# Head norm weights in the rotation tables, the query's root in the exponent, and the position bias loaded by GpSimd

## The chip, the cores and the metric

The kernel runs on one NeuronCore of one Trainium2 chip. All inputs and outputs lie in the chip's memory and are float32. The metric is the device time of one execution in microseconds (us), as the median of three runs. Five engines run their own instruction streams and meet only at semaphores: TensorE (PE), VectorE (DVE), ScalarE (ACT), GpSimd (POOL) and SyncE (SP). DMAs are issued by SP and by ACT in this kernel, and in the changed kernel by POOL too.

## The reference

Two blocks of layers over 256 tokens of width 2048. The first (a state space and linear attention mixer, then a squared ReLU MLP) is not touched. The second has two layers, each with three kinds of attention heads beside each other:

```python
def _layer(x, g_pre, g_post, w_in, a_qn, a_kn, ..., rpb, w_out, row, col):
    h = _rms_norm(x, g_pre)
    proj = einsum('bsd,de->bse', h, w_in)
    a_q, a_k, a_v, a_g, b_cq, b_ckv, b_kr, b_g, c_q, c_k, c_v, c_g = split(proj)
    # a: 8 query heads, 2 key heads of 128; norm by head, then rotation
    qa = _rope_axial(_rms_norm(a_q by head, a_qn), row, col)
    ka = _rope_axial(_rms_norm(a_k by head, a_kn), row, col)
    o_a = _dense_block_attention(qa, ka, a_v) * silu(a_g)
    # b: 4 heads whose queries, keys and values come out of two small latent rows
    o_b = _dense_block_attention(q_full, k_full, vb) * silu(b_g)
    # c: 4 heads, 16 neighbouring columns only, with a learnt position bias rpb
    o_c = _neighbourhood_attention(c_q, c_k, c_v, rpb) * silu(c_g)
    y = einsum('bse,ed->bsd', concat([o_a, o_b, o_c]), w_out)
    return x + _rms_norm(y, g_post)
```

`_rms_norm(x, g)` is x / sqrt(mean(x^2) + 1e-6) * g. `_rope_axial` turns the first half of a head's 128 numbers by the token's row and the second half by its column; in each half it is x * cos + (the two quarters exchanged) * (-sin, sin). The softmax is taken over scores times 128^-0.5.

## The kernel before

All large products are one stream of places. A place is a piece of 256 rows by 512 columns of a weight. SP loads it into one of four slots `raw`; ACT copies it to `w_hi` in a rounded format (L969), DVE subtracts to get the rest `w_lo` (L1600), and PE makes twelve matmuls of them (L939 to L941). Blocks of 512 output columns have 8 places in most weights, some have 1, 2, 6 or 16. ACT and DVE convert four places ahead of the place that they count (`AHEAD = 4`). A block's sums lie in two of four banks; they are taken out by ACT (L1507) and DVE (L2115, L2116) at place 3 of the next block (`DRAIN`), and PE may start the block after that only when both are done. SP loads into a slot again when DVE has split what was in it.

The rest of the work (attention, norms) stands beside this stream. Each piece of it is a generator that is started at a fixed place and goes on at fixed steps from there (`UNIT_STEP`, `ATTEND`), the same on every engine. So each engine's order is fixed in the program: at every place first the conversion four places ahead, then a drain if one is due, then the steps of the units beside. An engine that waits in such a step holds back all conversions behind it.

Each layer of the second block has four units, started 22 places apart: two of kind a (`grouped`, four query heads and one key head each, called a0 and a1 here), one of kind b (`latent_unit`) and one of kind c (`neighbour`).

In `grouped`, ACT issues seven loads: queries, key and value (L1421, L1423), the two norm weights (L1424, L1425), and the cos and sin tables (L1426, L1427). DVE waits for all of them at step 2, squares and sums (L1990, L1992, `root_of` L1609, L1611), ACT takes the roots (L983), at step 3 DVE multiplies by root and weight (L1998, L2000), at steps 4 and 6 it rotates one half of the tokens each (`rope`: L1982, L1985, L1987). At step 8 PE turns queries and keys (L789), at step 10 it makes the scores (L800), then DVE takes maxima (L2017, L2020), and ACT the exponentials (L1379).

In `neighbour`, ACT issues three loads of queries, keys and values (L1462), the load of the column mask (L1463) and sixteen loads of position bias out of a scratch tensor `skew` (L1467), each 64 partitions by four runs of 64 numbers, all at one place of its order. DVE waits for mask and bias at step 9 and adds them (L2091), and at step 10 adds the result to the scores (L2013). GpSimd has nothing to do but one memset near the start.

## Time and profile before

| | |
|---|---|
| median of 3 runs | 3020.25 us (3016.42 to 3022.92) |
| the profiled execution's own time | 3020.04 us |
| its span, first to last instruction | 3018.6 us |
| PE busy | 2932.7 us, 97% of the span |
| DVE busy | 1790.5 us, 59% |
| ACT busy | 1463.4 us, 48% |
| POOL busy | 0.4 us |
| mean granted TensorE clock | 0.984 of full speed |
| share of PE in the chain that ended last | 88% |

The busy figure of an engine counts instructions that run; an engine that issues DMAs or waits at a semaphore is idle by it. The clock is at one of two levels, full (1.0, 2.4 GHz) or half (0.5, 1.2 GHz), so a mean between them is a share of time at each. The profile's first 2190 us belong to the first block and the start of the second; the units of the first layer run from about 2212 to 2525 us, those of the second from about 2668 to 2980 us.

### The profile page before, as it was taken

To read this page: it belongs to the slowest core of one execution; us is meant where nothing else is said; L and a number is where in the kernel's file an instruction comes from. 1 tells how busy PE (TensorE), PEld (TensorE's weight loads), DVE (VectorE), ACT (ScalarE), POOL (GpSimd) and SP (SyncE) were. 2 spreads that over 40 slices of the span, in tenths; PEclk is the share of its full clock that TensorE was granted. 3 is DMA by queue.
4 is the path that set the end of the run, shared out by engine and by line. 5 is a ranking of instruction groups with operands and counts; after the bars stand their busy time and mean duration, and the time that the engine had idled before them with its cause. 6 is when DMAs were issued, how large, how long until landed. Compare 5 with 4: busy or idle time off the path is not lost.

```text
span 3018.6 us, 34820 instructions
## 1 busy us (share of the span) xinstructions
PE 2932.7 (97%) x13611; PEld 2428.2 (80%) x13611; DVE 1790.5 (59%) x2303; ACT 1463.4 (48%) x1997; POOL 0.4 (0%) x5
## 2 busy tenths in 40 slices
...
GB/s 209 223 210 224 229 220 228 236 228 225 251 224 229 230 227 257 276 217 163 222 196 177 202 176 201 171 196 136 240 204 199 195 213 175 234 207 191 207 202 164
DMA packets 348002, 634.99 MB, mean 210 GB/s; under 512 B 36653, under 2 KB 58413, under 8 KB 345534
## 3 DMA queue, kind: packets, MB, share of 16 engines
...
HBM read 582.99 MB, written 49.69 MB: 210 GB/s over the span
## 4 chain that ended last, share of the span: by engine, by line
PE 88%; DVE 5%; DMA 3%; ACT 2%; ACTq 2%; issue 1%; DVEq 0%
PE bank L939 27%; PE bank L941 27%; PE bank L940 27%; PE bank L601 2%; PE bank L800 1%; DMA arena<-in_sin 1%; DVE w_lo L1600 1%; PE bank L816 1%; PE bank L666 1%; ACTq L1467 1%; DMA raw<-in_w_out 1%; ACT w_hi L969 1%; PE bank L789 1%; DVE x_lo L1605 0%; PE bank L808 0%
## 5 line engine op out<-in xcount | busy, mean ns | idle before, releaser
L1600 DVE TENSOR_TENSOR w_lo<-raw,w_hi 128x1024 fp32r<-128x1024 f32 (+2 forms) x980 | 1159.4, 1206 | 732.2 <-ACT w_hi L969 721.6
L939 PE MATMUL bank<-w_lo,x_hi 128*128 128x512 f32 (+2 forms) x3920 | 1552.8, 396 | 34.1 <-DVE stage L2115 15.0
L941 PE MATMUL bank<-w_hi,x_lo 128*128 128x512 f32 (+2 forms) x3920 | 1529.6, 390 | 0.0
L940 PE MATMUL bank<-w_hi,x_hi 128*128 128x512 f32 (+2 forms) x3920 | 1529.5, 390 | 0.0
L969 ACT ACTIVATE w_hi<-raw 128x1024 fp32r<-128x1024 f32 (+2 forms) x980 | 993.3, 1045 | 735.7 <-PE bank L941 282.9
L939 PEld LDWEIGHTS bank<-w_lo,x_hi 128*128 128x128 f32 x3920 | 747.6, 191 | 190.9 <-DVE stage L2115 17.1
L941 PEld LDWEIGHTS bank<-w_hi,x_lo 128*128 128x128 f32 x3920 | 746.8, 191 | 152.7
L940 PEld LDWEIGHTS bank<-w_hi,x_hi 128*128 128x128 f32 x3920 | 747.6, 191 | 147.7 <-issue 2.9
L974 ACT ACTIVATE x_hi<-bank 128x512 fp32r<-128x512 f32 (+1 forms) x120 | 66.9, 589 | 329.2 <-PE bank L601 329.2
L1605 DVE TENSOR_TENSOR x_lo<-bank,x_hi 128x512 fp32r<-128x512 f32 (+1 forms) x120 | 78.1, 678 | 176.4 <-ACT x_hi L974 176.4
L601 PE MATMUL bank<-ident,arena 128*128 128x128 f32 x472 | 70.2, 288 | 29.8 <-DVE arena L1907 15.1
L601 PEld LDWEIGHTS bank<-ident,arena 128*128 128x128 f32 x472 | 58.6, 149 | 43.2 <-DVE arena L1907 18.3
L1675 DVE SCALAR_TENSOR_TENSOR arena<-arena 128x256 f32<-128x256 f32 x144 | 59.0, 478 | 45.3 <-ACT arena L1060 45.3
L983 ACT ACTIVATE arena<-arena 128x2 f32<-128x2 f32 (+2 forms) x38 | 7.5, 202 | 124.3 <-DVE arena L1611 103.2
L1385 ACT ACTIVATE arena<-bank 128x512 f32<-128x512 f32 x32 | 17.3, 593 | 59.0 <-PE bank L808 59.0
L800 PE MATMUL bank<-arena 128*128 128x256 f32 (+1 forms) x160 | 41.7, 398 | 0.0
L2030 DVE TENSOR_TENSOR arena<-arena 128x512 f32<-128x512 f32 x16 | 11.0, 688 | 50.6 <-ACT arena L1399 50.6
L1379 ACT ACTIVATE arena<-bank,arena 128x256 f32<-128x256 f32 x48 | 22.1, 482 | 33.6 <-DVE arena L2020 33.6
L1068 ACT ACTIVATE arena<-arena 128x128 f32<-128x128 f32 x128 | 38.2, 389 | 0.0
L800 PEld LDWEIGHTS bank<-arena 128*128 128x128 f32 (+1 forms) x160 | 27.8, 188 | 12.7 <-issue 10.0
L1369 ACT ACTIVATE arena<-bank 128x512 f32<-128x512 f32 (+3 forms) x34 | 16.4, 558 | 43.5 <-PE bank L789 43.5
L1055 ACT ACTIVATE arena<-bank 128x512 f32<-128x512 f32 x24 | 14.1, 586 | 42.9 <-PE bank L640 42.9
...
## 6 DMA issues: line engine op xcount, KB each, us to landing
...
raw<-in_w_up SPq DMA_DIRECT2D x128, 512.0 KB, 4.4
raw<-in_w_down SPq DMA_DIRECT2D x128, 512.0 KB, 4.6
...
```

What stands on the lines that cost most here:

```text
L601: op = pe.transpose(bank[b][:, k * P:(k + 1) * P], source[:, k * P:(k + 1) * P], ident[:, :])
L666: op = pe.matmul(bank[5 + t][:, h * SSD_P:(h + 1) * SSD_P], dec[:, t, h, :], xdt[:, t, h * SSD_P:(h + 1) * SSD_P], start=True, stop=True)
L800: op = pe.matmul(o_, qf(hh)[:, tokens(t)], kf(hh), start=(n == 0), stop=(n == len(parts) - 1))
L939: pe.matmul(o, x_hi[:, xk, tokens(t)], w_lo[:, r, k, 0:b.n], start=a, stop=False)
L940: pe.matmul(o, x_hi[:, xk, tokens(t)], w_hi[:, r, k, 0:b.n], start=False, stop=False)
L941: op = pe.matmul(o, x_lo[:, xk, tokens(t)], w_hi[:, r, k, 0:b.n], start=False, stop=z_)
L969: A(w_hi[:, p % SPLIT_RING, 0:b.per, 0:b.n], raw[:, p % RAW_RING, 0:b.per, 0:b.n], ACT.Copy).then_inc(*split_hi(p))
L974: return A(x_hi[:, x0:x0 + n, tokens(t)], full, ACT.Copy)
L1068: op = A(dec[:, t, h, :], dec[:, t, h, :], ACT.Relu, bias=gt[:, CS + t, h:h + 1], scale=-1.0)
L1600: TT(w_lo[:, p % SPLIT_RING, 0:b.per, 0:b.n], raw[:, p % RAW_RING, 0:b.per, 0:b.n], w_hi[:, p % SPLIT_RING, 0:b.per, 0:b.n].bitcast(F32), ...
L1605: return TT(x_lo[:, x0:x0 + n, tokens(t)], full, x_hi[:, x0:x0 + n, tokens(t)].bitcast(F32), ALU.subtract)
L1675: STT(cv[:, c, :], ut[:, c, w:w + S], cw[:, c, w:w + 1], cv[:, c, :], ALU.mult, ALU.add).then_inc(*ssd.dve("conv", g, w, c))
```

## The change

Four edits.

First, in `grouped` the norm weights are multiplied into cos and sin tables once per layer (`with_gain`, in unit a0 only), one pair of tables for queries and one for keys, and unit a1 uses them again. Norm weights, cos and sin are then loaded in a0 only; a1 loads queries, key and value.

Second, the queries are no longer multiplied by their root. The root of the queries is taken without the mean, so that it holds the factor 128^-0.5 too, and goes into the maxima (one `scalar_tensor_tensor` of 128x4) and into the exponentials' scale, which is now a number for each token and head. The keys are still multiplied by theirs. Keys are treated ahead of queries.

Third, the rotation's exchange (`rope`) is written by quarter, over all four heads at once: 4 instructions of 4x32 in place of 8 of 2x32 for queries, 4 of 32 in place of 2 of 2x32 for a key. The steps are one earlier: 3 and 5 in place of 4 and 6. Unit b uses the same function.

Fourth, mask and bias of `neighbour` are issued by GpSimd, after it has waited for the last readers and writers of that memory in unit b and for `skew`. DVE's wait is on their own semaphore.

```diff
@@ -434,6 +434,7 @@
+    bias_in = tally("bias_in", 16)
...
+            self.tables = {n: (room(NT, HD), room(NT, HD)) for n in "qk"}
@@ -1376,7 +1378,8 @@
-                    A(probs[t][:, hh, :], src, ACT.Exp, bias=small[:, t, hh:hh + 1], scale=1.0 if of_bias else scale,
+                    factor = 1.0 if of_bias else scale if scale else small[:, 4, t * UNIT_H + hh:t * UNIT_H + hh + 1]
+                    A(probs[t][:, hh, :], src, ACT.Exp, bias=small[:, t, hh:hh + 1], scale=factor,
                       accum_out=small[:, 2 + t, hh:hh + 1]).then_inc(*unit.act("exp", *key, t, hh))
@@ -1421,17 +1424,18 @@
-            act.dma_start(ga.gq, row_of(i["a_q_norm_2"][l], HD)).then_inc(*load[0]("unit", *key))
-            act.dma_start(ga.gk, row_of(i["a_k_norm_2"][l], HD)).then_inc(*load[0]("unit", *key))
-            act.dma_start(ga.cos, rows(i["cos128"])).then_inc(*load[0]("unit", *key))
-            act.dma_start(ga.sin, rows(i["sin128"])).then_inc(*load[0]("unit", *key))
+            if u == 0:
+                act.dma_start(ga.gq, row_of(i["a_q_norm_2"][l], HD)).then_inc(*load[0]("unit", *key))
+                act.dma_start(ga.gk, row_of(i["a_k_norm_2"][l], HD)).then_inc(*load[0]("unit", *key))
+                act.dma_start(ga.cos, rows(i["cos128"])).then_inc(*load[0]("unit", *key))
+                act.dma_start(ga.sin, rows(i["sin128"])).then_inc(*load[0]("unit", *key))
             yield UNIT_STEP["norm"] + 1
+            root_of(unit, (*key, "k"), small[:, 5, 0:2])
             root_of(unit, (*key, "q"), small[:, 4, :])
-            root_of(unit, (*key, "k"), small[:, 5, 0:2])
             yield UNIT_STEP["turn"]
             out_of_banks(("q", *key), ga.qt, (4, 5), HD)
             out_of_banks(("k", *key), ga.kt, (6,), HD)
-            yield from attend(key, UNIT_STEP["scores"], ga.probs, ga.pt, HD ** -0.5, False, ga.gate,
+            yield from attend(key, UNIT_STEP["scores"], ga.probs, ga.pt, None, False, ga.gate,
                               C2_AG + u * UW, KT + 4 * u)
 
@@ -1460,14 +1464,6 @@
-            act.dma_start(nu.mask, rows(i["window"])).then_inc(*load[1]("unit", *key))
-            for r in range(ROWS):
-                half = slice((r % 2) * GRID, (r % 2 + 1) * GRID)
-                for hh in range(C_H):
-                    act.dma_start(nu.bias[half, r // 2, hh * S:(hh + 1) * S].rearrange("p (a b) -> p a b", a=ROWS),
-                                  bass.AP(skew.tensor, (hh * DR + ROWS - 1 - r) * GRID * P + GRID - 1,
-                                          [[P - 1, GRID], [GRID * P, ROWS], [1, GRID]])).then_inc(
-                        *load[1]("unit", *key))
             yield UNIT_STEP["turn2"]
@@ -1978,30 +1974,35 @@
             xs, ts = split(x), split(tmp)
             ss = sin.rearrange("p (b s e) -> p b s e", b=2, s=2)
             for s in range(2):
-                for hh in range(heads):
-                    op = TT(ts[:, hh, :, s, :], xs[:, hh, :, 1 - s, :], ss[:, :, s, :], ALU.mult)
+                for b in range(2):
+                    op = TT(ts[:, :, b, s, :], xs[:, :, b, 1 - s, :], wide(ss[:, b, s, :].unsqueeze(1),
+                                                                           [P, heads, n // 4]), ALU.mult)
             op.then_inc(*unit.dve("shifted", *done))
             dve.wait_ge(*unit.dve.now)
             TT(x, x, wide(cos.unsqueeze(1), [P, heads, n]), ALU.mult).then_inc(*unit.dve("straight", *done))
             dve.wait_ge(*unit.dve.now)
             TT(x, x, tmp, ALU.add).then_inc(*unit.dve(*done))
 
-        def head_norm(key, x, n, g, stat, tmp):
+        def head_squares(key, x, stat, tmp):
             TT(tmp, x, x, ALU.mult).then_inc(*unit.dve("squares", *key))
             dve.wait_ge(*unit.dve.now)
             dve.tensor_reduce(stat, tmp, AX, ALU.add).then_inc(*unit.dve("sums", *key))
             dve.wait_ge(*unit.dve.now)
-            root_of(unit, key, stat, stat, HD, 1e-6)
-
-        def head_scale(key, x, n, g, stat):
-            dve.wait_ge(*unit.act["root", *key])
-            TT(x, x, wide(stat.unsqueeze(2), [P, n, HD]), ALU.mult).then_inc(*unit.dve("scaled", *key))
-            dve.wait_ge(*unit.dve.now)
-            TT(x, x, wide(g.unsqueeze(1), [P, n, HD]), ALU.mult).then_inc(*unit.dve("normed", *key))
+
+        def with_gain(l, name, gain):
+
+            cos, sin = ga.tables[name]
+            TT(cos, ga.cos, wide(gain.unsqueeze(1), [P, NT, HD]), ALU.mult).then_inc(*unit.dve("cos", l, name))
+            split = lambda a: a.rearrange("p t (b s e) -> p t b s e", b=2, s=2)
+            gains = gain.rearrange("p (b s e) -> p b s e", b=2, s=2)
+            for s in range(2):
+                for b in range(2):
+                    op = TT(split(sin)[:, :, b, s, :], split(ga.sin)[:, :, b, s, :],
+                            wide(gains[:, b, 1 - s, :].unsqueeze(1), [P, NT, HD // 4]), ALU.mult)
+            op.then_inc(*unit.dve("sin", l, name))
 
         def attend(key, at, probs, scale, bias, gate, x0):
             yield at
-            factor = 1.0 if bias is not None else scale
 
             def maxima(t):
                 top = small[:, t, 0:4]
@@ -2017,7 +2018,11 @@
                     op = dve.tensor_reduce(top[:, 2 * n:2 * n + 2], sc, AX, ALU.max)
                 op.then_inc(*unit.dve("top", *key, t))
                 dve.wait_ge(*unit.dve.now)
-                TS(top, top, -factor, None, ALU.mult).then_inc(*unit.dve("max", *key, t))
+                if scale:
+                    op = TS(top, top, -scale if bias is None else -1.0, None, ALU.mult)
+                else:
+                    op = STT(top, top, -1.0, small[:, 4, t * UNIT_H:(t + 1) * UNIT_H], ALU.mult, ALU.mult)
+                op.then_inc(*unit.dve("max", *key, t))
 
             def one_over_sums(t):
                 dve.wait_ge(*unit.act["exp", *key, t, 3])
@@ -2051,22 +2056,27 @@
             key = (l, "a", u)
             yield UNIT_STEP["norm"]
             dve.wait_ge(*load[0]["unit", *key])
-            norms = (((*key, "q"), heads_of(ga.q), NT * UNIT_H, ga.gq, small[:, 4, :], heads_of(ga.tmp)),
-                     ((*key, "k"), ga.k, NT, ga.gk, small[:, 5, 0:2], ga.tmp2[:, :, 0:HD]))
-            for n in norms:
-                head_norm(*n)
+            rq, rk = small[:, 4, :], small[:, 5, 0:2]
+            head_squares((*key, "k"), ga.k, rk, ga.tmp2[:, :, 0:HD])
+            root_of(unit, (*key, "k"), rk, rk, HD, 1e-6)
+            head_squares((*key, "q"), heads_of(ga.q), rq, heads_of(ga.tmp))
+            root_of(unit, (*key, "q"), rq, rq, 1, HD * 1e-6)
             yield UNIT_STEP["norm"] + 1
-            for n in norms:
-                head_scale(*n[:5])
+            if u == 0:
+                with_gain(l, "q", ga.gq)
+                with_gain(l, "k", ga.gk)
+            dve.wait_ge(*unit.act["root", *key, "k"])
+            TT(ga.k, ga.k, wide(rk.unsqueeze(2), [P, NT, HD]), ALU.mult).then_inc(*unit.dve("scaled", *key, "k"))
             dve.wait_ge(*unit.dve.now)
             for t in range(NT):
-                yield UNIT_STEP["norm"] + 2 + 2 * t
+                yield UNIT_STEP["norm"] + 1 + 2 * t
                 one = lambda a: a[:, t, :].rearrange("p (h n) -> p h n", n=HD)
-                rope(one(ga.q), UNIT_H, HD, ga.cos[:, t, :], ga.sin[:, t, :], one(ga.tmp),
-                     ("q", *key) if t else ("q0", *key))
-                rope(ga.k[:, t:t + 1, :], 1, HD, ga.cos[:, t, :], ga.sin[:, t, :], ga.tmp2[:, t:t + 1, 0:HD],
+                (cq, sq), (ck, sk) = ga.tables["q"], ga.tables["k"]
+                rope(one(ga.q), UNIT_H, HD, cq[:, t, :], sq[:, t, :], one(ga.tmp), ("q", *key) if t else ("q0", *key))
+                rope(ga.k[:, t:t + 1, :], 1, HD, ck[:, t, :], sk[:, t, :], ga.tmp2[:, t:t + 1, 0:HD],
                      ("k", *key) if t else ("k0", *key))
-            yield from attend(key, UNIT_STEP["scores"], ga.probs, HD ** -0.5, None, ga.gate, KT + 4 * u)
+            dve.wait_ge(*unit.act["root", *key, "q"])
+            yield from attend(key, UNIT_STEP["scores"], ga.probs, None, None, ga.gate, KT + 4 * u)
 
         def latent_unit(l):
             key = (l, "b", 0)
@@ -2085,7 +2095,7 @@
         def neighbour(l):
             key = (l, "c", 0)
             yield UNIT_STEP["scores"] - 1
-            dve.wait_ge(*load[1]["unit", *key])
+            dve.wait_ge(*bias_in[key[0]])
             for t in range(NT):
                 bt = nu.bias[:, t, :].rearrange("p (h n) -> p h n", h=C_H)
                 TT(bt, bt, wide(nu.mask[:, t, :].unsqueeze(1), [P, C_H, S]), ALU.add).then_inc(
@@ -2226,6 +2236,17 @@
         pool = nc.gpsimd
         pool.wait_ge(*start.pe["turned", 7])
         pool.memset(ones, 1.0).then_inc(*shared.pool("ones"))
+        for l in range(LAYERS):
+            pool.wait_ge(*unit.pe["turned_out", l, "b", 0, NT - 1])
+            pool.wait_ge(*unit.dve["out_lo", l, "b", 0, NT - 1])
+            pool.wait_ge(*side_out["skew", l])
+            pool.dma_start(nu.mask, rows(i["window"])).then_inc(*bias_in(l))
+            for r in range(ROWS):
+                half = slice((r % 2) * GRID, (r % 2 + 1) * GRID)
+                for hh in range(C_H):
+                    pool.dma_start(nu.bias[half, r // 2, hh * S:(hh + 1) * S].rearrange("p (a b) -> p a b", a=ROWS),
+                                   bass.AP(skew.tensor, (hh * DR + ROWS - 1 - r) * GRID * P + GRID - 1,
+                                           [[P - 1, GRID], [GRID * P, ROWS], [1, GRID]])).then_inc(*bias_in(l))
```

DVE's order in unit a1 of the first layer, from the norm to the last rotation. `w_lo<-raw,w_hi` is a place's conversion, `stage<-bank` a drain, `arena` holds everything of the unit. Before:

```order
L1992 TENSOR_REDUCE arena<-arena 128x2
L1609 TENSOR_SCALAR arena<-arena 128x2
L1611 RECIPROCAL arena<-arena 128x2
L1600 TENSOR_TENSOR w_lo<-raw,w_hi 128x1024
L1998 TENSOR_TENSOR arena<-arena 128x1024
L2000 TENSOR_TENSOR arena<-arena 128x1024
L1998 TENSOR_TENSOR arena<-arena 128x256
L2000 TENSOR_TENSOR arena<-arena 128x256
L1600 TENSOR_TENSOR w_lo<-raw,w_hi 128x1024
L1982 TENSOR_TENSOR arena<-arena 128x2x32 x8
L1985 TENSOR_TENSOR arena<-arena 128x512
L1987 TENSOR_TENSOR arena<-arena 128x512
```

The same place in the changed kernel (its line numbers are shifted; L1596 is the conversion, L2069 the key times its root, L1978 to L1984 the rotation):

```order
L1605 TENSOR_SCALAR arena<-arena 128x8
L1607 RECIPROCAL arena<-arena 128x8
L1596 TENSOR_TENSOR w_lo<-raw,w_hi 128x1024
L2069 TENSOR_TENSOR arena<-arena 128x256
L1978 TENSOR_TENSOR arena<-arena 128x4x32 x4
L1982 TENSOR_TENSOR arena<-arena 128x512
L1984 TENSOR_TENSOR arena<-arena 128x512
L1978 TENSOR_TENSOR arena<-arena 128x32 x4
L1982 TENSOR_TENSOR arena<-arena 128x128
L1984 TENSOR_TENSOR arena<-arena 128x128
L1596 TENSOR_TENSOR w_lo<-raw,w_hi 128x1024 x2
L2126 COPY stage<-bank 128x256
```

Three multiplications stand no more between the norm and the rotation, and the first rotation comes ahead of the second conversion. The second rotation (not shown) follows the drain directly; before, a conversion stood between.

DVE's order in unit a0 of the first layer, where the tables are made, before:

```order
L2115 TENSOR_SCALAR stage<-bank,arena 128x512
L1998 TENSOR_TENSOR arena<-arena 128x1024
L2000 TENSOR_TENSOR arena<-arena 128x1024
L1998 TENSOR_TENSOR arena<-arena 128x256
L2000 TENSOR_TENSOR arena<-arena 128x256
L1600 TENSOR_TENSOR w_lo<-raw,w_hi 128x1024
```

And after, with L1995 and L2000 for the tables:

```order
L2125 TENSOR_SCALAR stage<-bank,arena 128x512
L1995 TENSOR_TENSOR arena<-arena 128x256
L2000 TENSOR_TENSOR arena<-arena 128x2x32 x4
L1995 TENSOR_TENSOR arena<-arena 128x256
L2000 TENSOR_TENSOR arena<-arena 128x2x32 x4
L2069 TENSOR_TENSOR arena<-arena 128x256
```

The tables stand where the four multiplications stood, behind the same drain; the rotation follows them with no conversion between.

ACT's order where unit c of the first layer begins, before (L969 is a place's conversion, L1507 ACT's part of a drain):

```order
L969 ACTIVATE w_hi<-raw 128x1024 x3
L1462 DMA arena<-proj 128x2x512 x3
L1463 DMA arena<-in_window 128x2x256
L1467 DMA arena<-skew 64x4x64 x16
L969 ACTIVATE w_hi<-raw 128x1024
L1507 ACTIVATE stage<-bank,arena 128x512
```

And after (L971 is the conversion, L1503 the drain):

```order
L971 ACTIVATE w_hi<-raw 128x1024 x3
L1466 DMA arena<-proj 128x2x512 x3
L971 ACTIVATE w_hi<-raw 128x1024
L1503 ACTIVATE stage<-bank,arena 128x512
L971 ACTIVATE w_hi<-raw 128x1024 x2
```

Seventeen DMA issues have left ACT's queue; conversion and drain follow the three loads directly.

## Rows read from the trace of the kernel before

**Rows 1.** Page, part 1: busy time, share of the span and instructions.

```profile
PE 2932.7 (97%) x13611; PEld 2428.2 (80%) x13611; DVE 1790.5 (59%) x2303; ACT 1463.4 (48%) x1997; POOL 0.4 (0%) x5
```

**Rows 2.** PE's waits, 2060 us to the end: us in total, times, longest.

```profile
PE bank L939 <- DVE stage L2115: 15.0, 6, 4.7
PE bank L789 <- DVE arena L1987: 11.0, 2, 5.6
```

**Rows 3.** Timeline of PE, after idle time: start, us, instruction [idle before, releaser].

```profile
2231.79 0.50 PE L939 MATMUL bank<-w_lo,x_hi 128*128 128x512 f32 x1 [2.89 <-DVE stage L2115]
...
2321.68 2.40 PE L789 MATMUL bank<-ident,arena 128*128 128x128 f32 x10 [5.45 <-DVE arena L1987]
...
2464.28 0.50 PE L939 MATMUL bank<-w_lo,x_hi 128*128 128x512 f32 x1 [4.57 <-DVE stage L2115]
...
2686.15 0.50 PE L939 MATMUL bank<-w_lo,x_hi 128*128 128x512 f32 x1 [2.16 <-DVE stage L2115]
...
2768.78 0.50 PE L939 MATMUL bank<-w_lo,x_hi 128*128 128x512 f32 x1 [1.02 <-DVE w_lo L1600]
...
2777.37 2.40 PE L789 MATMUL bank<-ident,arena 128*128 128x128 f32 x10 [5.58 <-DVE arena L1987]
...
2920.89 0.79 PE L939 MATMUL bank<-w_lo,x_hi 128*128 128x512 f32 x1 [4.71 <-DVE stage L2115]
```

**Rows 4.** Stretches behind gaps: length, busy by engine (count), PEclk, DMA share, GB/s.

```profile
2321.68:2325.68 4.00, 4.00 (x17) 3.64 (x18) 3.07 (x6) 1.99 (x4) 0.00 (x0) 0.62 0.60 173
2464.28:2469.28 5.00, 5.00 (x15) 3.97 (x16) 3.97 (x4) 2.61 (x3) 0.00 (x0) 0.66 0.92 265
2777.37:2783.37 6.00, 6.00 (x22) 5.22 (x23) 4.72 (x8) 3.32 (x6) 0.00 (x0) 0.60 0.74 228
2920.89:2926.89 6.00, 6.00 (x17) 4.77 (x18) 4.58 (x4) 2.61 (x3) 0.00 (x0) 0.62 0.82 273
2231.79:2236.79 5.00, 5.00 (x15) 3.96 (x16) 4.20 (x5) 4.54 (x7) 0.00 (x0) 0.66 0.66 210
```

**Rows 5.** Timeline of DVE in unit a1 of the first layer.

```profile
2303.40 1.23 DVE L1990 TENSOR_TENSOR arena<-arena 128x1024 f32<-128x1024 f32 x1 [3.72 <-DMA arena<-in_sin]
...
2308.51 1.22 DVE L1998 TENSOR_TENSOR arena<-arena 128x1024 f32<-128x1024 f32 x1
2309.76 1.23 DVE L2000 TENSOR_TENSOR arena<-arena 128x1024 f32<-128x1024 f32 x1
...
2311.35 0.43 DVE L2000 TENSOR_TENSOR arena<-arena 128x256 f32<-128x256 f32 x1
...
2319.01 1.16 DVE L1982 TENSOR_TENSOR arena<-arena 128x64 f32<-128x64 f32 x8
2320.21 0.69 DVE L1985 TENSOR_TENSOR arena<-arena 128x512 f32<-128x512 f32 x1
```

**Rows 6.** DMA issues, 2284 to 2334 us: count, KB each, us to landing.

```profile
arena<-proj ACTq DMA_DIRECT2D x2, 128.0 KB, 4.4
...
arena<-in_sin ACTq DMA_DIRECT2D x1, 128.0 KB, 10.2
```

**Rows 7.** Timelines of ACT and DVE where unit c of the first layer begins.

```profile
2446.94 14.21 ACTq L1467 DMA_DIRECT2D arena<-skew x16
2461.25 1.06 ACT L969 ACTIVATE w_hi<-raw 128x1024 fp32r<-128x1024 f32 x1 [14.35 <-issue]
...
2463.49 0.74 DVE L2115 TENSOR_SCALAR stage<-bank,arena 128x512 f32<-128x512 f32 x1
```

**Rows 8.** Line L1467, issue ns min/median/max, and its DMAs' time to landing.

```profile
L1467 ACTq DMA_DIRECT2D arena<-skew x32: 587/642/2284, 2446.9 to 2917.1; - x32
...
DMA to landing us min/median/max: 2.3/5.4/9.9
```

**Rows 9.** Timeline of DVE, mask and bias added, and the next use.

```profile
2482.91 2.35 DVE L2091 TENSOR_TENSOR arena<-arena 128x1024 f32<-128x1024 f32 x2
...
2490.50 0.69 DVE L2013 SCALAR_TENSOR_TENSOR arena<-bank,arena 128x512 f32<-128x512 f32 x1 [3.97 <-PE bank L800]
```

## The prediction

> **What bounds the kernel now.** Read the page's busy times first [rows 1]: PE is busy for 2932.7 of 3018.6 us, so 86 us of PE's idle time is all that can be won without touching its work, beside what a half clock costs. PE's instructions are the same in both kernels. DVE at 59% and ACT at 48% matter only where PE waits for them. So the second view is PE's waits [rows 2]: 15.0 us for the drain L2115 in six waits, 11.0 us for the rotation L1987 in two. The third is PE's timeline around them [rows 3]: in each layer one gap at the start of unit a0 (2.89 and 2.16 us), one where unit a1's queries are turned (5.45 and 5.58 us, with 1.02 us just ahead of the second), and one at the start of unit c (4.57 and 4.71 us). The fourth is the granted clock behind each gap [rows 4]: it stands between 0.60 and 0.66 over the four to six microseconds after PE goes on, so part of them is at 1.2 GHz. A stretch of length L at mean clock c loses (1 - c) x L of full speed time.
>
> **Unit a1 (loads, root, tables, rotation).** The gap of 5.45 us ends when DVE has added the second half's queries (L1987, right after the L1985 of 2320.21) [rows 3, 5]. PE came to it at 2321.68 - 5.45 = 2316.2. What DVE did too late, in the first layer:
> - Its norm began at 2303.40, after 3.72 us of idle time that the sin table ended [rows 5]. DVE was free at 2299.7. The sin table took 10.2 us to land; key and value, which are still loaded, took 4.4 us [rows 6], and are issued ahead of it. So the norm starts at 2299.7: 3.7 us won.
> - Queries times root (1.22 us), queries times weight (1.23 us) and keys times weight (0.43 us) go [rows 5]: 2.9 us with the time between them.
> - The exchange: 8 instructions of 64 take 1.16 us together, 0.145 us each [rows 5]. Four of 128 and, for the key, four of 32 in place of two of 64 have no row. If an instruction's time is fixed, four cost 0.6 us; if it goes by elements, 1.16 us. I take 0.85 us for queries and 0.5 for the key (two of 64 would be 0.3): together 0.1 us less than before, at worst 0.3 us more. The key's two products of 128 lie between 0.145 (64) and 0.43 us (256); I take 0.3 each.
> - The second rotation moves one place up and one conversion (1.2 us) goes behind it.
>
> The norm takes 4.0 us (2303.40 to 2308.51, less one conversion of 1.2 us, as long as the products of 1024 [rows 5]). DVE then runs: norm 2299.7 to 2303.7, conversion to 2304.9, key times root to 2305.3, first rotation (0.85 + 0.7 + 0.7, key 0.5 + 0.3 + 0.3) to 2308.7, two conversions and the drain of 256 columns (0.4) to 2311.5, second rotation of queries to 2313.8, of the key to 2314.9. PE comes at 2316.2. It is 2.4 us ahead for queries and 1.3 for the key, so the wait goes, and no other takes its place by this count. In the second layer PE waited 1.02 us for a conversion as well, one place ahead of the gap of 5.58 us [rows 3]: DVE is late by more there, and wins the same. Won: 5.45 + 5.58 + 1.02 = 12.05 us of gaps, and by rows 4 (1 - 0.62) x 4 + (1 - 0.60) x 6 = 3.9 us of half clock. Term: **-16.0 us**. The roots are taken by ACT in the other order, but ACT still waits for the later of the two; the scale of the exponentials is read from memory now. A drain with such a scale takes DVE 0.74 us against 0.69 for a product of the same 512 [rows 7, 5]; I take 0.1 us for each of eight exponentials in a unit (0 to 0.2), beside a PE that waits for none of them.
>
> **Unit a0.** It keeps its seven loads and DVE's wait for the last. The drain L2115 stands behind the same norm as before, so the gaps of 2.89 and 2.16 us stay. Behind the drain come two table products of 256 (0.43 each), eight of 64 (0.145 each), and the key's root (0.43), against 3.3 us of multiplications that go: 2.4 against 3.3 us. But the first rotation (3.4 us) comes ahead of the next conversion, so that one ends near 2239, some 2 us later. PE begins its block at 2231.79 and needs it four places on. A place takes about 3 us (from 2768.78 to 2771.79, where the next gap begins [rows 3]), so at 2243.8, and 1.7 us later by the half clock [rows 4]. Five us of cover; term 0. If the cover were gone it would cost 2 us a layer.
>
> **Unit b.** Rotation in half the instructions, no PE wait there: 0.
>
> **Unit c (bias issued by GpSimd).** ACT stands at L1467 for 14.21 us, its next conversion says "issue" for 14.35 us, DVE's drain L2115 follows at 2463.49 and PE at 2464.28 [rows 7, 3]. Without the issues ACT goes on at 2446.5. The drain's sums are complete one block of six places, 16 to 18 us, before PE's stop at 2464.28 - 4.57 = 2459.7, so by 2443. Conversion (1.06 and 1.2 us) and drain end near 2450, ten us ahead of PE. Won: 4.57 + 4.71 = 9.28 us of gaps, and (1 - 0.66) x 5 + (1 - 0.62) x 6 = 4.0 us of half clock [rows 4]. Term: **-13.3 us**.
>
> What it adds: DVE's mask addition L2091 waits for 17 DMAs of GpSimd. Queued behind it are the conversions, and PE behind these. GpSimd waits for what ACT's first load waits for, and four issues of some 0.5 us stand between that and 2446.94 [rows 7], so it can begin at 2444.9. L2091 started at 2482.91 [rows 9] and will want to start 6.3 us earlier, at 2476.6: 31.7 us. After it DVE has 3.97 us of idle time before L2013 [rows 9], and beyond that PE's scores are late. With c us for each DMA and 5.4 us to land [rows 8], DVE waits from c = (31.7 - 5.4) / 17 = 1.55 us on, and PE is held from (31.7 + 4.0 - 5.4) / 17 = 1.78 us on. No DMA of GpSimd is in the trace. From below, ACT issues the fastest of these in 0.587 us; from above, if GpSimd made one at a time to its landing, 5.4 us [rows 8]. Nearest is ACT's own mean for the same sixteen, 14.21 / 16 = 0.89 us [rows 7]: the last lands at 2444.9 + 15.1 + 5.4 = 2465.4. I take that, and no wait.
>
> The Trainium skill's page "DMA: Bandwidth & Descriptors", section "Issuing engines are not separate DMA queues", says that all engines' DMAs interleave on the same 16 DMA engines, and that issuing from several engines only saves the sequencer's time, usually small beside the DMA. By that the unit c term would be near 0, and the sum 3020 - 16 = 3004. This trace has the issue time at 14.2 us against 5.4 us to land [rows 7, 8], so here the sequencer's time is the large one. The part on the shared engines stands, and is the second rival's mechanism.
>
> The same page's section "Anatomy of one DMA" fits a GpSimd DMA at 2.0 us plus its bytes at 436 GB/s: for 64 KB an estimate of 2.15 us. If they ran one after the other at that, PE would be held 6 us in each layer, with 2 us of half clock, and the sum would be about 3008; it also says most of the 2 us is the wait for completion, which overlapping DMAs share. No GpSimd DMA here shows it yet.
>
> **Sum.** 3020.04 - 16.0 - 13.3 = 2990.8 us. I give back 1.2 us for waits on conversions like the 1.02 us one that a PE without gaps may meet. **Forecast 2992 us**, 28 us (0.93%) less than the profiled execution's 3020.04, which is within 0.2 us of the median of 3020.25.
>
> **Rivals.**
> - *More (2983.5).* The gaps at unit a0 go as well, 2.89 + 2.16 us and 1.7 us of half clock each. For it: nothing but the key's norm standing first. Against: the same loads, the same wait. From the forecast, 2992 - 8.5 = 2983.5.
> - *One term comes back (3006).* PE without its gap finds conversions late: either DVE's rotation ends after 2316 since small strided instructions cost more, or the bias, now read beside the weights that ACT's stall had held back, delays a weight at unit c. For it: the margins in a1 are 1.3 and 2.4 us. Against: four converted places, some 11 us, lie between DVE and PE at unit c. It gives 2992 + 13 to 2992 + 16, 3005 to 3008.
> - *The change does not do what it says for the bias.* GpSimd's DMAs take between 1.78 and 2.5 us each: PE waits for the mask, up to the whole gain: 2992 to 3020.
> - *Slower: GpSimd cannot make the DMAs in time.* At L2091 DVE stands, conversions stop, PE runs dry. Each microsecond per DMA is 17 us in each of two layers. With 2 us of half clock per gap it decides at c = 1.78 + (28 / 2 - 2) / 17 = 2.5 us. At 3.5 us the time is 2992 + 2 x (1.72 x 17 + 2) = 3054; at 5.4 us, one at a time to landing, 3119. For it: no row shows GpSimd's price. Against: ACT's DMAs of the same shape overlap.
>
> **How the numbers follow.** Forecast 0.62; more 0.08; one term back 0.18; bias late but not slower 0.06; slower 0.06. A difference under 0.2% (6 us) can't be told from none. Faster holds the forecast, more, one term back and half of the late bias: 0.90, lowered by the doubt of the unseen engine to 0.89; same 0.05; slower 0.06. The range 2983 to 3008 takes in the forecast, one term back and nearly all of more: 0.85. The unknown costs move the forecast little inside it: the exchange between its bounds is 0.4 us on a path with 1.3 us of room, GpSimd anywhere from 0.587 to 1.78 us is no PE wait. Its own range is 2986 to 2998, since where the half clock falls moves by a few us when all gaps shift.
>
> **What would show it.** Right: L789 in a1 has no idle time before it; DVE's first square in a1 starts right behind its conversion; ACT's conversion follows L1466's three loads in 2 to 3 us; PE's waits for the drain fall from 15.0 us to about 5, all at a0; mask addition starts without a wait on the bias; mean clock above 0.984. Wrong: a PE wait at the mask or at unit c's scores, GpSimd's seventeenth DMA landing later than 31.7 us after unit b's last x_lo, or new PE waits on `w_lo`.

## The result, and the profile after

The changed kernel takes 2986.76 us (median of 4 runs, 2984.37 to 2992.48); the kernel before took 3021.3 us beside it (4 runs, 3016.42 to 3022.92). The ratio is 0.9894 with a 95% interval of 0.9877 to 0.9911: about 1.1% faster, 34.5 us by the medians. The profiled execution took 2987.2 us, 32.8 us less than the 3020.04 of before; its span is 2985.7 us and its mean granted clock 0.988 (before 3018.6 us and 0.984). The forecast was 2992 us.

The page's busy times, which answer to [rows 1]:

```profile
PE 2922.4 (98%) x13611; PEld 2421.1 (81%) x13611; DVE 1780.9 (60%) x2287; ACT 1466.3 (49%) x1997; POOL 21.6 (1%) x39
```

PE runs the same 13611 instructions and is busy 10.3 us less: that part of the gain is clock, and the other 22.6 us of the span's 32.9 are waits. GpSimd has 21.6 us of work now, for its 34 DMAs. PE's waits from 2060 us to the end, which answer to [rows 2]:

```profile
PE bank L603 <- DVE arena L1903: 15.2, 11, 3.0
PE bank L941 <- DVE arena L2199: 6.6, 2, 4.5
PE bank L941 <- DVE stage L2125: 4.2, 2, 2.2
```

L791, the turning that was L789, is gone from the list (11.0 us before). The drain, once L2115 and now L2125, went from 15.0 us in six waits to 4.2 us in two, both in unit a0. The others were there before. PE's timeline at the places of [rows 3]: the drain of a0, the turning in a1 and in unit c, then the same a0 and a1 places in the second layer.

```profile
2228.14 0.50 PE L941 MATMUL bank<-w_lo,x_hi 128*128 128x512 f32 x1 [2.17 <-DVE stage L2125]
...
2311.76 1.26 PE L791 MATMUL bank<-ident,arena 128*128 128x128 f32 x10
...
2456.32 1.91 PE L791 MATMUL bank<-ident,arena 128*128 128x128 f32 x16
...
2668.35 0.50 PE L941 MATMUL bank<-w_lo,x_hi 128*128 128x512 f32 x1 [2.03 <-DVE stage L2125]
...
2751.96 1.26 PE L791 MATMUL bank<-ident,arena 128*128 128x128 f32 x10
```

No bracket stands behind the three turnings. Ten of them took 2.40 us in a1 before, at half clock behind the gap [rows 3], and take 1.26 us now. The windows behind PE's a1 turning and behind the a0 drain:

```profile
2311.76:2315.76 4.00, 4.00 (x24) 3.48 (x23) 1.77 (x3) 2.92 (x5) 0.00 (x0) 1.00 0.92 286
2228.14:2233.14 5.00, 5.00 (x15) 3.98 (x16) 4.86 (x22) 4.54 (x7) 0.00 (x0) 0.66 0.68 210
```

PEclk is 1.00 where it was 0.62, and 24 matmuls fit in four microseconds where 17 did [rows 4]. Behind the a0 drain the gap stays and so does the 0.66.

One marker, the start of PE's turning in each unit, says where the time came from. In the first layer the changed kernel is ahead by 3.64 us in a0, 9.92 in a1, 11.41 in b and 17.86 in c; in the second by 17.79, 25.41, 27.66 and 34.8; at the end of the span by 32.9. The difference from a0 to b is what unit a1 won: 7.8 us and 9.9 us, 17.6 together (the working: 11.41 - 3.64, and 27.66 - 17.79). From b to c it is 6.5 and 7.1 us, 13.6 together. The remaining 1.7 us lie elsewhere: some 3.6 us ahead of and inside the first a0, less 2 us behind the last marker.

Most of that rest is nothing the change did. Matched matmul by matmul, the two executions are level near 1390 us (0.1 us apart), 2.7 us apart at 1401, and still 2.9 at 2225, ahead of the first a0. And the 2 us behind the last marker are lost in one stretch, 2962.5 to 2966.5 us, where the changed kernel's granted clock is 0.57. In the first block, which the change leaves alone, PE waits 3.05 us near 1393.8 us in both executions. The rows of before, and its window behind them:

```profile
1393.81 1.09 PE L601 MATMUL bank<-ident,arena 128*128 128x128 f32 x4 [3.05 <-DVE arena L1897]
```

```profile
1393.00:1403.00 10.00, 9.19 (x32) 7.27 (x32) 3.78 (x5) 3.19 (x5) 0.00 (x0) 0.66 0.19 54
```

And of after:

```profile
1393.87 0.63 PE L603 MATMUL bank<-ident,arena 128*128 128x128 f32 x4 [3.05 <-DVE arena L1893]
```

```profile
1393.00:1403.00 10.00, 8.39 (x40) 6.74 (x41) 6.53 (x8) 4.99 (x6) 0.00 (x0) 1.00 0.32 81
```

The same wait was followed by a clock of 0.66 in one execution and of 1.00 in the other. In those ten microseconds PE did 32 matmuls at the one and 40 at the other. So a difference of 2 or 3 us between two kernels here says nothing, and a cost of half clock behind a given gap is an expectation, not a certainty.

DVE in unit a1 of the first layer, which answers to [rows 5]:

```profile
2284.75 1.29 DVE L1601 TENSOR_TENSOR x_lo<-bank,x_hi 128x512 fp32r<-128x512 f32 x2 [3.74 <-ACT x_hi L976]
2286.19 4.63 DVE L1596 TENSOR_TENSOR w_lo<-raw,w_hi 128x1024 fp32r<-128x1024 f32 x4
2290.91 0.75 DVE L2125 TENSOR_SCALAR stage<-bank,arena 128x512 f32<-128x512 f32 x1
2293.51 1.23 DVE L1596 TENSOR_TENSOR w_lo<-raw,w_hi 128x1024 fp32r<-128x1024 f32 x1 [1.85 <-ACT w_hi L971]
2294.65 0.42 DVE L1987 TENSOR_TENSOR arena<-arena 128x256 f32<-128x256 f32 x1
...
2306.14 0.88 DVE L1978 TENSOR_TENSOR arena<-arena 128x128 f32<-128x128 f32 x4
...
2307.79 0.69 DVE L1984 TENSOR_TENSOR arena<-arena 128x512 f32<-128x512 f32 x1
2308.40 0.49 DVE L1978 TENSOR_TENSOR arena<-arena 128x32 f32<-128x32 f32 x4
...
2309.25 0.29 DVE L1984 TENSOR_TENSOR arena<-arena 128x128 f32<-128x128 f32 x1
```

The key's norm starts at 2294.65 with nothing between it and the conversion, 8.6 us after the last x_lo (2284.75 + 1.29 = 2286.04). Before, that was 13.7 us. The queries are done at 2308.5 and the key at 2309.5; PE comes at 2311.76, so there are 3.3 and 2.2 us of room.

GpSimd in unit c, ACT there, which answers to [rows 7], and then DVE's mask addition, which answers to [rows 9]:

```profile
2434.12 0.85 POOL L2243 DMA_DIRECT2D arena<-in_window  x1 [2421.99 <-DVE x_lo L1601]
2434.96 9.85 POOL L2247 DMA_DIRECT2D arena<-skew  x16
```

```profile
2435.39 1.06 ACT L971 ACTIVATE w_hi<-raw 128x1024 fp32r<-128x1024 f32 x1
2436.34 0.68 ACT L1503 ACTIVATE stage<-bank,arena 128x512 f32<-128x512 f32 x1
2445.90 1.06 ACT L971 ACTIVATE w_hi<-raw 128x1024 fp32r<-128x1024 f32 x1 [8.88 <-DMA raw<-in_w_out]
```

```profile
2465.04 2.36 DVE L2101 TENSOR_TENSOR arena<-arena 128x1024 f32<-128x1024 f32 x2
```

GpSimd's sixteen take 9.85 us, 0.62 us each, against ACT's 14.21 us for the same [rows 7]. A single issue costs about the same on both, 0.667 and 0.642 us in the median; ACT's longest took 2.284 us, GpSimd's 0.719 [rows 8, and below]. From the first issue to the last landing it is 16 us either way: 2434.96 to 2451.22 by GpSimd, 2446.94 to 2462.85 by ACT. The line of L2247 by its source, with its DMAs' time to landing (answers to [rows 8]):

```profile
L2247 POOL DMA_DIRECT2D arena<-skew x32: 627/667/719, 2435.0 to 2884.1; - x32
...
DMA to landing us min/median/max: 6.5/7.2/7.6
```

The last lands at 2451.22, nearly 14 us before DVE adds the mask, and DVE has no wait there. ACT drains at 2436.34 right behind its conversion. What is new at this place is the wait of 8.88 us of ACT for a weight. SP's four weight loads of 2434.9 to 2438.3 us, and the time to landing:

```profile
L2262 SPq DMA_DIRECT2D raw<-in_w_out x4: 367/368/368, 2434.9 to 2438.3; - x4
...
DMA to landing us min/median/max: 11.0/14.8/15.3
```

Over the whole run a weight takes 4.7 us in the median, and none takes longer than 15.3. These four are in flight beside the bias, the mask and ACT's three loads of 512 KB; how much of the delay is the bias's alone was not measured. Waits of ACT as long, 9.97 us at 2517.95, stand at places without a bias too. PE has no wait from it.

### The profile page after: what moved, and what is told of

It reads as the page before. It is cut to its first block, busy times and chain, and to the rows that moved or that the text cites. A ratio compares the mean times of both kernels' runs of the same rounds, so it can differ in the third digit from the quotient of the medians.

```text
span 2985.7 us, 34798 instructions
## 1 busy us (share of the span) xinstructions
PE 2922.4 (98%) x13611; PEld 2421.1 (81%) x13611; DVE 1780.9 (60%) x2287; ACT 1466.3 (49%) x1997; POOL 21.6 (1%) x39
## 4 chain that ended last, share of the span: by engine, by line
PE 91%; DVE 3%; DMA 3%; ACT 1%; issue 1%; ACTq 0%; DVEq 0%
PE bank L941 28%; PE bank L943 28%; PE bank L942 28%; PE bank L603 2%; PE bank L802 1%; DVE w_lo L1596 1%; PE bank L818 1%; PE bank L668 1%; DMA raw<-in_w_out 1%; ACT w_hi L971 1%; DMA arena<-in_sin 1%; PE bank L810 0%; PE bank L791 0%; PE bank L642 0%; DVE x_lo L1601 0%
## 5 line engine op out<-in xcount | busy, mean ns | idle before, releaser
L1596 DVE TENSOR_TENSOR w_lo<-raw,w_hi 128x1024 fp32r<-128x1024 f32 (+2 forms) x980 | 1158.4, 1206 | 722.4 <-ACT w_hi L971 711.0
L971 ACT ACTIVATE w_hi<-raw 128x1024 fp32r<-128x1024 f32 (+2 forms) x980 | 993.1, 1044 | 714.4 <-PE bank L943 278.4
L1382 ACT ACTIVATE arena<-bank,arena 128x256 f32<-128x256 f32 x48 | 24.9, 537 | 30.4 <-DVE arena L2022 19.2
```

The costliest lines, as they stand in the source:

```text
L971: A(w_hi[:, p % SPLIT_RING, 0:b.per, 0:b.n], raw[:, p % RAW_RING, 0:b.per, 0:b.n], ACT.Copy).then_inc(*split_hi(p))
L1596: TT(w_lo[:, p % SPLIT_RING, 0:b.per, 0:b.n], raw[:, p % RAW_RING, 0:b.per, 0:b.n], w_hi[:, p % SPLIT_RING, 0:b.per, 0:b.n].bitcast(F32), ...
```

## The experiments

The time of each stands as its median, and as the ratio to the kernel before run beside it with the 95% interval.

**GpSimd's issue alone.** The kernel before with only the fourth edit (that hunk of the diff above, nothing of `grouped`, `rope` or `with_gain`).

> The kernel before with the fourth edit alone: mask and bias issued by GpSimd. Theory (ACT's 14.2 us of issues hold drain and conversions, and nothing else ties them to unit a1): the waits of 4.57 and 4.71 us at unit c go with their half clock, those of 5.45 and 5.58 us at unit a1 stay. Time 13.3 us less than before, about 3007 us. Rival (the terms share slack, so that either edit alone brings more or less than its part of the 34.5 us measured for both): over 17 us or under 9 us less.

3005.86 us, 0.9945 (0.9932 to 0.9958); the profiled execution was the shortest of six, 2999.99 us. Unit c's waits are gone. PE's timeline in a1 of both layers:

```profile
2319.74 2.39 PE L790 MATMUL bank<-ident,arena 128*128 128x128 f32 x10 [5.58 <-DVE arena L1980]
...
2765.11 2.29 PE L790 MATMUL bank<-ident,arena 128*128 128x128 f32 x10 [4.48 <-DVE arena L1980]
```

The waits of a1 stay, 10.1 us in place of 11.0.

**The other three edits alone**, mask and bias issued by ACT again:

```diff
+            act.dma_start(nu.mask, rows(i["window"])).then_inc(*load[1]("unit", *key))
+            for r in range(ROWS):
...
-            dve.wait_ge(*bias_in[key[0]])
+            dve.wait_ge(*load[1]["unit", *key])
```

> The changed kernel with mask and bias issued by ACT again, all at one place as before. Theory: L791 in unit a1 has no idle time ahead of it, unit c has its waits of 4.6 us with their half clock. Time 16 to 19 us less than before, 3002 to 3005 us. Rival (terms share slack): the two parts e1 and e2 add up to less than 27 us or more than 38 us.

3001.1 us, 0.9936 (0.9922 to 0.9949). No wait in a1, and unit c's are back, 5.38 us in the first layer and 4.83 in the second:

```profile
2453.74 0.80 PE L940 MATMUL bank<-w_lo,x_hi 128*128 128x512 f32 x1 [5.38 <-DVE stage L2132]
```

By the ratios the one half gives 0.55% and the other 0.64%, and both together 1.06%. The halves add, within the intervals.

**Bias and loads**: the first of these kernels with the four table loads in a0 only, all of DVE's old work kept.

```diff
-            act.dma_start(ga.gq, row_of(i["a_q_norm_2"][l], HD)).then_inc(*load[0]("unit", *key))
...
+            if u == 0:
+                act.dma_start(ga.gq, row_of(i["a_q_norm_2"][l], HD)).then_inc(*load[0]("unit", *key))
...
```

> e1 with the four loads of norm weights and tables in unit a0 only; all multiplications and rotations as in the kernel before. It tells apart what the loads and what the DVE work are worth in unit a1. Theory: DVE's norm starts 3.7 us (first layer) and about 5 us (second) earlier, the waits of 5.45 and 6.6 us shrink to about 1.7 us each, and the half clock behind them may go: 9 to 13 us less than e1, so 2994 to 2998 us. Rival (DVE's work is what counts, the landing of the tables is hidden): under 4 us less than e1. Second rival (the loads are all of it): as fast as the changed kernel, 2987 us.

2987.87 us (2986.76 to 2989.86), 0.9887 (0.9873 to 0.9901). The theory missed: without any of the removed arithmetic it is as fast as the changed kernel. PE's waits in a1:

```profile
2310.24 1.36 PE L790 MATMUL bank<-ident,arena 128*128 128x128 f32 x10 [0.91 <-DVE arena L1981]
...
2753.12 1.36 PE L790 MATMUL bank<-ident,arena 128*128 128x128 f32 x10 [1.00 <-DVE arena L1981]
```

1.9 us are left of 11.0, and ten turnings take 1.36 us, so no half clock stands behind them. Why the loads alone do that is seen on ACT. First the kernel before, then this one:

```profile
2291.65 0.49 ACTq L1424 DMA_DIRECT2D arena<-in_a_q_norm  x1
...
2293.19 0.53 ACTq L1427 DMA_DIRECT2D arena<-in_sin  x1
2293.82 1.06 ACT L969 ACTIVATE w_hi<-raw 128x1024 fp32r<-128x1024 f32 x1 [2.12 <-PE bank L941]
```

```profile
2285.42 1.06 ACT L970 ACTIVATE w_hi<-raw 128x1024 fp32r<-128x1024 f32 x1
```

The four issues hold ACT for 2 us, and the conversion behind them feeds DVE. DVE's norm starts 8.5 us after the last x_lo (x_lo ends at 2283.46, norm at 2291.95) in place of 13.7: 5.2 us, of which DVE's wait for the sin table is 3.7; the rest is 1.58 us that DVE waited for ACT ahead of its fourth conversion, and no longer does.

**All loads again**: the changed kernel with the four loads in a1 too (the `if u == 0` taken away from them).

> The changed kernel with the four loads put back into unit a1 (they bring the same numbers again). Theory: DVE's norm starts 3.7 and about 5 us later again, the queries' second rotation ends about 1 us (first layer) and 3 us (second) after PE comes to it: 4 us of PE waits, and up to 3.4 us of half clock: 2990 to 2995 us. Rival (the work saved is enough by itself): 2987 us, no wait of PE at L791 in unit a1. Second rival (the loads are all of it): 2999 us or more.

2995.86 us (2986.56 to 2998.51, 5 runs), 0.9914 (0.9899 to 0.9929). The time is near what was said, by a median over a wide spread. The profiled execution was one of the short ones. In it the norm waits for the sin table:

```profile
2296.97 0.43 DVE L1986 TENSOR_TENSOR arena<-arena 128x256 f32<-128x256 f32 x1 [4.19 <-DMA arena<-in_sin]
```

Yet PE waits for 0.71 and 0.67 us only at the turning, less than the 4 us expected. But this execution had the highest clock of the five, 0.991 against 0.987 to 0.989, which is worth 6 to 12 us of the 7 to 12 us between it and the others (an estimate from the spans: the share of lost clock times the span). What made the clock fall in them is not in this trace. By the medians of kernels that ran side by side, the loads alone bring 18 us over GpSimd's issue alone (3005.86 to 2987.87), the other edits without the loads 10 us (3005.86 to 2995.86). So the two savings overlap, and the loads are the larger one. Once they are gone, taking the arithmetic away as well brings nothing: 2987.87 us with all of it, 2986.76 without (0.9887 and 0.9894 by the ratios).

**The steps of before**: rotations at steps 4 and 6 again.

```diff
-                yield UNIT_STEP["norm"] + 1 + 2 * t
+                yield UNIT_STEP["norm"] + 2 + 2 * t
```

> The changed kernel with the rotations at steps 4 and 6 again. One conversion of 1.2 us comes ahead of each rotation that stood behind it. Theory: in the changed kernel the second half's queries are done about 3 us ahead of PE, so 1 to 2 us later makes no wait: same time as the changed kernel, 2987 us. Rival (the earlier step is what saved it): a wait of PE of 1 us or more at L791 in unit a1 in each layer, 2990 us or more.

2986.25 us, 0.9891 (0.9875 to 0.9908), no wait in a1. The earlier steps are worth nothing. In this execution (2992.38 us, the longest of four) a0's drain waits are 3.29 and 4.22 us, against 2.17 and 2.03 in the changed kernel; over the kernels here that leave ACT's issue and DVE's one wait in a0 as they were, the two together range from 3.1 to 7.5 us. So a single trace doesn't give them to better than that.

**The rotation of before**: exchange by head in place of by quarter.

```diff
-                for b in range(2):
-                    op = TT(ts[:, :, b, s, :], xs[:, :, b, 1 - s, :], wide(ss[:, b, s, :].unsqueeze(1),
-                                                                           [P, heads, n // 4]), ALU.mult)
+                for hh in range(heads):
+                    op = TT(ts[:, hh, :, s, :], xs[:, hh, :, 1 - s, :], ss[:, :, s, :], ALU.mult)
```

> The changed kernel with the exchange written by head again: 8 of 64 for queries in place of 4 of 128, 2 of 64 for the key in place of 4 of 32. Theory: one rotation costs 1.17 + 0.35 us in place of 0.90 + 0.49 us, 0.13 us more, hidden in 3 us of room: same time, 2987 us, the same PE waits to 0.3 us. Rival (the rewriting brought a part of the gain): 2 us or more above the changed kernel.

2986.18 us, 0.9896 (0.9881 to 0.991), no wait in a1. That rewriting is worth nothing here either.

**Bias by ACT, spread** over four steps, four DMAs at each:

```diff
+            for r in range(ROWS):
+                yield r + 1
...
+                    act.dma_start(nu.bias[half, r // 2, hh * S:(hh + 1) * S].rearrange("p (a b) -> p a b", a=ROWS),
```

> The changed kernel with mask and bias issued by ACT, four of the sixteen at each of four places in turn. Theory (what cost was that ACT stood 14 us at one place, more than the four places of conversions ahead cover with the drain behind it): each group holds ACT 3 to 4 us, the drain at unit c comes in time, no wait of PE there: 2987 to 2990 us. Rival (only an engine with nothing else to do can issue them): a wait of PE of 2 us or more at unit c, 2993 us or more.

2989.36 us, 0.9902 (0.9887 to 0.9918), no wait at unit c. It was not GpSimd that won unit c's term, but that the sixteen issues no longer stand ahead of one conversion in one piece.

**Late bias**: the changed kernel with 160 memsets of GpSimd (33.5 us) ahead of its DMAs.

```diff
+            for n in range(160):
+                pool.wait_ge(*shared.pool.now)
+                pool.memset(idle[:, :], 1.0).then_inc(*shared.pool("idle", l, n))
```

> The changed kernel with 160 small memsets on GpSimd ahead of its loads in each layer, which hold them back by some 20 to 40 us (read from the trace). It stands for a slow GpSimd and tests the slower rival of the prediction. In the changed kernel the last bias lands about 13 us before DVE's mask addition. Theory: with a delay of D us DVE waits D - 13 us at the mask, PE is held by D - 17 us (4 us of room behind the mask), plus 1.7 us of half clock for each layer: at D = 30 about 2987 + 2 x (13 + 1.7) = 3016 us. Rival (four converted places hide DVE's wait from PE up to about 11 us): at D = 30 no more than 2987 + 2 x 6.

3001.03 us, 0.9942 (0.9927 to 0.9957). DVE's mask addition in the first layer, then PE's wait behind it (7.05 us in the second layer):

```profile
2477.79 2.36 DVE L2102 TENSOR_TENSOR arena<-arena 128x1024 f32<-128x1024 f32 x2 [14.29 <-DMA arena<-skew]
```

```profile
2486.41 1.97 PE L811 MATMUL bank<-ident,arena 128*128 128x128 f32 x8 [7.25 <-ACT arena L1383]
```

The theory missed: it said 3016 us, and the rival, that converted places hide much of DVE's wait from PE, at most 2999. The slower rival's mechanism of the prediction exists, with two corrections. PE is held at the turning of the probabilities, by ACT's exponentials, and not by missing conversions. And DVE can be late by 14.29 - 7.25 = 7.0 us before PE is, not by 4.0. Put into the rival's own formula with the forecast's landing of 5.4 us, PE would be held from (31.7 + 7.0 - 5.4) / 17 = 1.96 us per DMA on. GpSimd took 0.62. The sixteen also land faster here than the 7.2 us of the changed kernel. In the first layer SP issues no weight between 2463.5 and 2481.4 us, as DVE frees no slot:

```profile
DMA to landing us min/median/max: 2.2/2.4/3.6
```

**Own wait**: the changed kernel, where a0's four table loads have their own semaphore, and DVE waits for it only ahead of the table products.

```diff
-                act.dma_start(ga.sin, rows(i["sin128"])).then_inc(*load[0]("unit", *key))
+                act.dma_start(ga.sin, rows(i["sin128"])).then_inc(*table_in(l))
...
             if u == 0:
+                dve.wait_ge(*table_in[l])
                 with_gain(l, "q", ga.gq)
```

> The changed kernel, in which unit a0 waits for norm weights and tables on a semaphore of their own, ahead of the table products and no longer ahead of the norm. Theory (the waits of 2.17 and 2.03 us for the drain at unit a0 come from the norm's wait for the sin table): the norm starts 4 to 5 us earlier there, both waits and their half clock go: 7.6 us less than the changed kernel's 2986.8, about 2979 us. Rival (the drain is late for ACT's sake, since seven issues stand ahead of its conversion): waits of PE at the drain of 1 us or more stay, under 3 us less.

2977.6 us (2973.65 to 2979.34), 0.9859 (0.9839 to 0.9878): it beats both kernels, and is 9 us below the changed one's median (they did not run side by side; each ratio is to the kernel before beside it, and the intervals just touch). Both drain waits of a0 are gone. DVE's first square, first of the changed kernel and then of this one:

```profile
2222.24 0.42 DVE L1987 TENSOR_TENSOR arena<-arena 128x256 f32<-128x256 f32 x1 [4.25 <-DMA arena<-in_sin]
```

```profile
2216.00 0.42 DVE L1988 TENSOR_TENSOR arena<-arena 128x256 f32<-128x256 f32 x1 [1.46 <-DMA arena<-proj]
```

**Own wait, old work**: GpSimd's bias and the own semaphore in both units, with all loads by ACT and all the old arithmetic.

> e1 (bias by GpSimd, old multiplications and rotations) in which all seven loads are still issued by ACT in both units, but norm weights and tables are waited for on their own semaphore ahead of the scaling. e3 without these loads brought 18 us over e1; that holds DVE's wait for them and 2 us of ACT's issue time with what it delays. Theory (DVE's wait is most of it): the norm starts right behind its conversion, 2 to 4 us of PE waits stay in unit a1 over both layers, and unit a0's wait for the drain goes: 2984 to 2992 us. Rival (ACT's issue time and the conversions it delays are most of it): 2996 us or more, with PE waits of 3 us or more at L790 in unit a1.

2985.68 us, 0.9892 (0.9876 to 0.9908): a time like the changed kernel's, though with more of PE's waits left in a1 than the 2 to 4 us that were said (the profiled execution was the longest of five, 2993.63 us):

```profile
2315.19 1.36 PE L791 MATMUL bank<-ident,arena 128*128 128x128 f32 x10 [2.67 <-DVE arena L1981]
```

With the second layer's 3.92 us that is 6.6 us, between the 10.1 us of GpSimd's issue alone and the 1.9 us of the kernel where the loads were left out. So in these executions the shared semaphore is the smaller part of what the loads cost in a1. The rest differs by layer. DVE in the first, then ACT in the second:

```profile
2302.00 1.23 DVE L1992 TENSOR_TENSOR arena<-arena 128x1024 f32<-128x1024 f32 x1 [0.92 <-DMA arena<-in_sin]
```

```profile
2735.36 1.06 ACT L971 ACTIVATE w_hi<-raw 128x1024 fp32r<-128x1024 f32 x1 [4.15 <-DMA raw<-in_w_in]
```

In the first, DVE still waits 0.92 us for the sin table, and its norm starts 10.3 us after the last x_lo in place of 8.5: conversion and drain stood behind ACT's issues. In the second, the norm starts 11.7 us after it in place of 8.6, and most of that is a weight which lands late beside the four loads (ACT waits 4.15 us for it; without the loads 1.69). So issue time and the loads' own traffic both count. The a0 waits, gone here, pay for it.

**Tables by GpSimd**: own wait, with a0's four loads issued by GpSimd.

```diff
+            pool.wait_ge(*unit.pe["latent", l, 0, NT - 1])
+            pool.wait_ge(*unit.dve["latent_lo", l, 0, NT - 1])
+            pool.wait_ge(*side_out["skew", l])
+            pool.dma_start(ga.gq, row_of(i["a_q_norm_2"][l], HD)).then_inc(*table_in(l))
...
```

> e9 with the four loads of unit a0 issued by GpSimd. Theory: ACT is free 2 us earlier at unit a0, GpSimd's four land before the table products need them; as fast as e9 or up to 2 us faster, 2977 to 2979 us. Rival (GpSimd's loads land too late or hold the weights back): a new wait at unit a0, slower than e9 by 2 us or more.

2990.43 us, 0.9904 (0.9887 to 0.992): 13 us slower than with ACT's issue. The theory missed, and a0's drain waits are back with 4.92 and 4.41 us. GpSimd issued them at 2193.7, 16 us ahead of ACT's load of the queries at 2210.0. Was it the time, or the engine? So:

**Tables by GpSimd, later**: it also waits for the stores that ACT's three loads wait for.

```diff
+            for b in (start_of["dram", "proj2", C2_AK, l], start_of["dram", "proj2", C2_AQ, l]):
+                for s in both_landed(b):
+                    pool.wait_ge(*s)
```

> As the kernel in which GpSimd issues unit a0's four loads and DVE waits for them separately, but GpSimd also waits for the stores that ACT's three loads wait for. So they start beside the queries, near 13 us later (2206.5 in place of 2193.7). Theory: in the kernel before it the early loads crowded the weight loads and ACT's conversions; without that no weight is late, the drain in a0 has no PE wait, and the time is that of the kernel with its own wait, 2975 to 2980 us. Rival: it is GpSimd's loads beside the queries that hurt, whenever they start; then the queries land late, DVE's norm starts after 2220, the drain waits of 4 to 5 us stay and the time is 2986 to 2992 us.

2995.5 us (2994.47 to 2998.47), 0.9919 (0.9906 to 0.9931): slower still. The rival's mechanism is right (drain waits in a0, 5.78 and 5.75 us, and a norm after 2220), though it said at most 2992 us; an early start was not the harm. The DMA view of 2190 to 2225 us (queue: packets, MB, share of 16 engines; issues: KB each, median us to landing), first of the own-wait kernel, then of this one:

```profile
q10 hardware_dynamic: 2287, 2.42, 24.3%
...
raw<-in_w_in SPq DMA_DIRECT2D x11, 512.0 KB, 4.8
...
arena<-proj ACTq DMA_DIRECT2D x2, 128.0 KB, 7.6
```

```profile
q10 hardware_dynamic: 1362, 1.86, 14.5%
q0 software_dynamic: 160, 0.39, 8.2%
...
raw<-in_w_in SPq DMA_DIRECT2D x10, 512.0 KB, 7.3
...
arena<-proj ACTq DMA_DIRECT2D x2, 128.0 KB, 12.1
```

Key and value take 12.1 us to land in place of 7.6, the weights 7.3 in place of 4.8. DVE's norm starts at 2226.57 in place of 2216.00; as this whole execution runs 4 us later there (SP's load of `in_b_w_ukv` starts at 2204.09 and 2200.06), some 6.5 us of that are the loads'. GpSimd's 0.39 MB take 8.2% of the engines' time, and ACT's queue takes 9.8% less: together it is no more than before. That these loads from GpSimd go with slow landings of everything beside them is shown; by what mechanism is open. One rival stands untested: GpSimd's four were issued ahead of ACT's three (from 2206.26 on), ACT's four behind them, and ACT issuing them in the earlier order was not tried.

## Why the prediction was right, and where it was not

The mechanism was right: PE's waits in a1 and c go, those in a0 stay, and nothing takes their place. 32.8 us between the profiled executions against 28 forecast.

- *Term a1, -16.0.* Measured 17.6 by the markers. The waits went as said. The steps toward it were sized too small in one place: the norm was to start right behind its conversion, 10.0 us after the last x_lo, and it starts 8.6 us after it. The 2 us that ACT spends on issuing four loads stood ahead of a conversion, and the prediction took only DVE's wait for the last of them out; the other 1.4 us it left in. The issues of a removed load count as well as its landing. The room ahead of PE is 3.3 and 2.2 us for it, against 2.4 and 1.3.
- *What carried the term* was not told apart by the forecast, and the experiments are its correction. It listed the wait (3.7 us), the arithmetic (2.9), the exchange and the steps as if each were needed. The loads alone leave 1.9 us of PE's wait in both layers and bring all of the term in time (18 us); the other edits alone leave 1.4 us in the execution profiled, the one of the highest clock, and bring 10 us in the median. The exchange and the steps carry nothing, and the arithmetic nothing beside the loads.
- *Exchange*: 0.85 us for 4x128 and 0.5 for 4x32 were taken; 0.88 and 0.49 are measured. "At worst 0.3 us more" was not met. The exponentials with a scale out of memory take 0.08 us more each (0.562 in place of 0.478 us in the median of L1382 and L1379), where 0.1 was taken, and no PE wait comes of it.
- *Term c, -13.3.* Measured 13.6. GpSimd's price was the unknown: 0.89 us per DMA taken from ACT's mean, 0.62 measured; landing 5.4 taken, 7.2 measured. It began at 2434.12, and would want the mask at 2465.04: 30.9 us, where the prediction had 31.7. The last landed nearly 14 us ahead, where 2476.6 - 2465.4 = 11 was said.
- *What ACT was spared.* The trace agrees with the first half of what the Trainium skill's "DMA: Bandwidth & Descriptors", section "Issuing engines are not separate DMA queues", states, that all DMAs share the engines: weights issued beside the bias took 11.0 to 15.3 us to land, against 4.7 in the median. It does not agree with the second, that the sequencer's time is usually small: that time was worth 0.55% here, and spreading it over steps was worth the same.
- The Trainium skill's 2.0 us plus bytes for a GpSimd DMA ("DMA: Bandwidth & Descriptors", section "Anatomy of one DMA") would, for DMAs one after another, have given 3008, by the prediction's estimate. The sixteen were issued in 9.85 us and landed 6.5 to 7.6 us after their issue, so they overlap, and that rival falls.
- *Unit a0, 0.* 2.17 and 2.03 us remain of 2.89 and 2.16, a difference within what these waits vary by. Right; and the own-wait kernel shows that the wait for the sin table was its cause.
- *Give-back, +1.2.* Nothing of it was met; PE's waits on `w_lo` went from 4.2 to 3.2 us.
- *The rest*: 32.8 is 17.6 + 13.6 + 1.7 within rounding; the 1.7 lies outside the changed units, where half clock fell in one execution and not in the other.
- *Slower rival*: real, but it decides far from what GpSimd does. Its room of 4.0 us behind the mask was read from DVE's idle time; 7.0 us is what PE showed.
- *Slips of the working.* The norm's 4.0 us is 3.9 by its own rows (2308.51 - 2303.40 - 1.2), and the chances named for "faster" add up to 0.91, not 0.90. Neither moves the forecast.
